# Attention of the second layer in a fused fp32 block: value product with split values stationary and two query blocks moving

## What is computed

```python
    def block(args):
        qn, qr = args
        s = (jnp.einsum('bqhd,bkhd->bhqk', qn, k_nope)
             + jnp.einsum('bqhd,bkd->bhqk', qr, k_rope)).astype(jnp.float32) * scale
        p = jax.nn.softmax(s, axis=-1).astype(v.dtype)
        return jnp.einsum('bhqk,bkhd->bqhd', p, v)
    ...
    y = o * jax.nn.silu(gate)
    return y @ w_out
```

## Time and profile before

| What | us |
|---|---|
| median of 3 runs (4584.55 to 4600.62) | 4598.31 |
| the profiled execution, its own time | 4581.67 |
| its span, first to last instruction | 4579.9 |
| PE busy (95% of the span) | 4337.8 |
| DVE busy | 1856.7 |
| ACT busy | 1277.5 |
| POOL busy | 1281.5 |
| the loop over blocks of the stage, from the first score matmul to the end of the last scores' issue (1191.1 to 1783.3) | 592.2 |
| from there to the first matmul of the output projection (1803.9) | 20.6 |

### The profile page before, as it was taken

How to read it: one execution, slowest core, us unless ns; L and a number is a source line. 1 busy time by engine, 2 the same in 40 slices (tenths; PEclk the granted TensorE clock), 3 DMA queues, 4 the chain that set the end, 5 groups by cost and what they waited for, 6 DMA issues and landing times.

```text
span 4579.9 us, 51693 instructions
## 1 busy us (share of the span) xinstructions
PE 4337.8 (95%) x20631; PEld 3531.6 (77%) x20631; DVE 1856.7 (41%) x3427; ACT 1277.5 (28%) x2692; POOL 1281.5 (28%) x1225
## 2 busy tenths in 40 slices
PE   8999999798999999899888999999999888999998
PEld 4969788477899998787556888887786566888887
DVE  2020210455355554612754343334514734333434
ACT  1120211213344443312543322112313533312222
POOL 1403120145100000632123444334332042433431
PEclk9959689699999999999988999999998998999999
DMA  5101012422100000310013111112210022111112
GB/s 184 54 23 42 23 37 70 145 96 69 41 7 8 8 8 28 104 48 23 1 44 102 46 56 47 47 46 70 97 43 13 1 67 98 48 47 44 56 49 97
DMA packets 224513, 244.67 MB, mean 53 GB/s; under 512 B 43848, under 2 KB 165208, under 8 KB 224272
## 3 DMA queue, kind: packets, MB, share of 16 engines
q1 hardware_dynamic: 190432, 162.78, 12.0%
q10 hardware_dynamic: 33840, 78.58, 4.9%
HBM read 209.10 MB, written 30.07 MB: 52 GB/s over the span
## 4 chain that ended last, share of the span: by engine, by line
PE 84%; DVE 9%; ACT 3%; issue 1%; DMA 1%; POOL 1%; SPq 0%; ACTq 0%; DVEq 0%; POOLq 0%
PE ps L127 79%; PE ps L130 5%; DVE tlo L139 1%; DVE cst_sm L150 1%; DVE tfi L147 1%; ACT m_junk L133 0%; POOL mix_z L139 0%; DVE m_hb L147 0%; ACT f_ta L133 0%; DVE m_z L147 0%; ACT thi L133 0%; DVE gt_yr L139 0%; DVE m_z L139 0%; DVE c_rn L139 0%; DVE tfl L147 0%
## 5 line engine op out<-in xcount | busy, mean ns | idle before, releaser
L136 POOL CAST whi<-wst 128x512 fp32r<-128x512 f32 (+3 forms) x562 | 389.9, 694 | 2767.0 <-DMA wst<-in_a_w_in 561.2
L139 POOL TENSOR_TENSOR wlo<-wst,whi 128x512 fp32r<-128x512 f32 (+3 forms) x562 | 733.7, 1306 | 45.0
L127 PE MATMUL ps<-thi,whi 128*128 128x512 f32 x1760 | 692.2, 393 | 14.0 <-ACT m_z L133 5.6
L127 PE MATMUL ps<-tlo,whi 128*128 128x512 f32 x1760 | 690.5, 392 | 0.0
L127 PE MATMUL ps<-thi,wlo 128*128 128x512 f32 x1760 | 689.8, 392 | 0.0
L127 PE MATMUL ps<-whi,thi 128*128 128x512 f32 (+3 forms) x1752 | 670.1, 382 | 3.5 <-DVE mix_z L139 2.6
L127 PE MATMUL ps<-wlo,thi 128*128 128x512 f32 (+3 forms) x1752 | 665.3, 380 | 0.0
L127 PE MATMUL ps<-whi,tlo 128*128 128x512 f32 (+3 forms) x1752 | 664.9, 379 | 0.0
L147 DVE SCALAR_TENSOR_TENSOR f_ta<-f_ua,tfi,f_ta 128x1024 f32<-128x1024 f32 x88 | 120.6, 1371 | 736.7 <-ACT f_ta L133 735.1
L127 PEld LDWEIGHTS ps<-whi,thi 128*128 128x128 f32 x1752 | 370.5, 211 | 50.7 <-DVE mix_z L139 3.0
L127 PEld LDWEIGHTS ps<-whi,tlo 128*128 128x128 f32 x1752 | 370.1, 211 | 47.3
(11 more groups left out here) (266 smaller groups left out, 6145.0 us busy)
## 6 DMA issues: line engine op xcount, KB each, us to landing
wst<-in_w_up SPq DMA_DIRECT2D x704, 64.0 KB, 2.0
wst<-in_ada_w SPq DMA_DIRECT2D x96, 256.0 KB, 3.6
wst<-in_w_down SPq DMA_DIRECT2D x88, 256.0 KB, 2.6
wst<-in_a_w_in SPq DMA_DIRECT2D x96, 192.0 KB, 2.4
wst<-in_w_in SPq DMA_DIRECT2D x64, 256.0 KB, 2.7
wst<-in_w_out SPq DMA_DIRECT2D x32, 256.0 KB, 4.6
m_xr<-scr_x ACTq DMA_DIRECT2D x16, 512.0 KB, 3.6
scr_x<-m_z ACTq DMA_DIRECT2D x16, 512.0 KB, 2.7
```

Source lines behind the costliest of these rows:

```text
L127: return self.none if self.e is None else self.e.matmul(*a, **k)
L136: return self.none if self.e is None else self.e.tensor_copy(*a)
L139: return self.none if self.e is None else self.e.tensor_tensor(*a)
```

## The change

- **Value product.** The values are stationary: for each 128 keys a 128x128 square with the 64 columns of the high part beside the 64 of the low part (`bv`). The transposed weights of two blocks, a pair, are moving, 256 columns wide, once their high part (`pth`) and once their low part (`ptl`): 16 matmuls of 128x256 in fp32r for a pair. The result is transposed, values by queries; rows 0 to 63 come from the high values, 64 to 127 from the low.
- **Evacuation of a turn.** ACT copies both halves (the high parts), and DVE subtracts for both halves (the low parts). Before, each engine copied one half.
- **Order.** The value product of a pair is issued in even iterations, behind that iteration's scores. A turn of an even block stands behind the value product, a turn of an odd block at the head of the next, odd iteration, in front of the scores.
- **Gate.** POOL multiplies the gate by the reciprocal of the sum (one 128x64 TENSOR_SCALAR a block). PE transposes two gate squares a pair into the bank of the output. ACT copies 64 rows of the bank (one half of the output, and the gate) to `ot`, DVE adds the other half, POOL multiplies by the gate into `tfl`. The output is then already transposed, so the 64 squares at the end go; 16 copies by ACT and 16 subtractions by DVE of 128x512 split it, and `pe_out` waits for the k-th of them at its k-th step.
- **Smaller.** The scale moves into the query table, so TENSOR_SCALAR goes and the maximum is written negated. The low part of a query piece is made by POOL and the queries have one buffer `qs` in place of two. Value pieces stand two iterations later and are split in two copies and two subtractions each. The waits for the gate's DMAs move from the start of ACT's and DVE's programs to the first low part of a turn. POOL splits 11 of the 16 weight tiles of the output projection within the loop.

```diff
-    c["k_qtab"] = tab
+    c["k_qtab"] = tab * f(96.0 ** -0.5)
...
+        self.bv = [[x[:, 4 * hf:4 * hf + 4, :] for hf in range(2)] for x in v] + [[four(self.thi[:, 7, half(hf)]) for hf in range(2)]]
+
+        self.pth = [four(self.thi[:, 8, :]), self.place("ml5_p0", [128, 4, 256], F32R, mod)[:]]
...
-                self.split(q, ("wo", st, h, k))
+                if st != "b" or 8 * h + k > 10:
+                    self.split(q, ("wo", st, h, k))
...
     def pool_heads(self, q):
-        for h in range(16):
+        S = self.S
+        for h in range(2):
             self.split(q, ("head", h))
+        for piece in self.first_pieces():
+            self.pool_piece_lo(q, *piece)
+        for i in range(128 + 7):
+            if i and self.piece_at(i - 1):
+                self.pool_piece_lo(q, *self.piece_at(i - 1))
+            if i % 8 == 0 and i < 112:
+                self.split(q, ("head", i // 8 + 2))
+            if i % 8 == 4 and 40 <= i < 128:
+                n = i // 8 - 5
+                self.split(q, ("wo", "b", n // 8, n % 8))
+            if i >= 5 and i % 2 == 1 and i < 133:
+                p = (i - 5) // 2
+                y, o, r = self.head_out(p)
+                q.wait_ge(*self.B.done(("bo", p)))
+                q.wait_ge(*S.last("b_gate"))
+                q.wait_ge(*S.last("w_lo"))
+                q.wait_ge(*S.last("lo_p"))
+                q.tensor_tensor(y, o[:, 0:256], o[:, 256:512], ALU.mult).then_inc(*S.up("b_y", p))
+                q.wait_ge(*S.at("b_y", p))
+            if 1 <= i < 129:
+                u = i - 1
+                h, j = u // 8, u % 8
+                g = self.tfl[:, h // 2 + 1, j * 128 + 64 - h % 2 * 64:j * 128 + 128 - h % 2 * 64]
+                q.wait_ge(*S.at("b_rec", u))
+                if h == 0:
+                    q.wait_ge(*S.at(f"ld_g{j}"))
+                q.tensor_scalar(g, g, self.bstat(u, 2), None, ALU.mult).then_inc(*S.up("b_gate", u))
...
     def pieces(self, h):
-        return [("q", 0), ("k", 0), ("q", 1), ("k", 1)] + ([("v", 0), ("v", 1)] if h % 2 == 0 else [])
+        return [("q", 0), ("k", 0), ("q", 1), ("k", 1)] + ([None, None, ("v", 0), ("v", 1)] if h % 2 == 0 else [])
...
+            for n in range(2):
+                if h + n >= 3:
+                    q.wait_ge(*S.at("pv", ("b", 4 * (h + n - 3) + 3)))
+                ins = q.activation(self.bv[(h + n) % 3][hf][:, :, 0:64], p.rearrange("p (a b) -> p a b", a=4)[:, :, 64 * n:64 * n + 64],
+                                   ACT.Copy)
+            ins.then_inc(*S.up("hi", key))
...
+            if (h, hf) != (0, 0):
+                q.wait_ge(*S.at("hi", ("piece", h if hf else h - 1, what, 1 - hf)))
+                q.wait_ge(*S.at("lo_p", ("hq", h if hf else h - 1, 1 - hf)))
+            q.tensor_tensor(self.qs[:], p, self.msh[:, r], ALU.mult).then_inc(*B.free(key, "evac_v"))
...
+        else:
+            q.wait_ge(*S.at("hi", key))
+            for n in range(2):
+                v = self.bv[(h + n) % 3][hf]
+                ins = q.tensor_tensor(v[:, :, 64:128], p.rearrange("p (a b) -> p a b", a=4)[:, :, 64 * n:64 * n + 64],
+                                      v[:, :, 0:64].bitcast(F32), ALU.subtract)
+            ins.then_inc(*B.free(key, "evac_v"))
...
+    def pool_piece_lo(self, q, h, what, hf):
...
-        q.tensor_tensor(self.ql[x][:, r], self.qs[hf][:], self.qh[x][:, r].bitcast(F32), ALU.subtract).then_inc(
-            *self.S.up("lo", ("hq", h, hf)))
+        q.tensor_tensor(self.ql[x][:, r], self.qs[:], self.qh[x][:, r].bitcast(F32), ALU.subtract).then_inc(
+            *self.S.up("lo_p", ("hq", h, hf)))
...
+        for i in range(128 + 4):
+            if i % 2 == 1 and i >= 3:
+                self.pe_head_turn(q, i - 2)
...
-            if 2 <= i < 130:
-                for n in range(2):
-                    self.pe_turn(q, ("bt", i - 2, n), [self.bp[(i - 2) % 3][:, blk(4 * n + k)] for k in range(4)], "t2",
-                                 [S.at("exp", ("b", i - 2))])
-            if i < 120 and i % 8 < len(self.pieces(i // 8 + 1)):
-                self.pe_piece(q, i // 8 + 1, *self.pieces(i // 8 + 1)[i % 8])
-            if 3 <= i < 131:
-                u = i - 3
-                h = u // 8
-                key = ("bo", u)
+            if i == 2:
+                self.pe_head_turn(q, 0)
+            if i >= 4 and i % 2 == 0:
+                p = (i - 4) // 2
+                h, n = p // 4, p % 4
+                key = ("bo", p)
                 b = B.take(key, "o2")
                 for event in B.freed(key):
                     q.wait_ge(*event)
-                v = self.bv[h // 2 % 2]
-                for k in range(8):
-                    q.wait_ge(*B.done(("bt", u, k // 4)))
-                    q.wait_ge(*B.done(("piece", h // 2 * 2, "v", k // 4)))
-                    ins = q.matmul(ps[:, b, 0:64], self.bpt[u % 2][:, blk(k)], v[:, k, h % 2 * 64:h % 2 * 64 + 64],
-                                   start=(k == 0), stop=(k == 7))
-                ins.then_inc(*S.up("pv", ("b", u)))
-        for j in range(8):
+                q.wait_ge(*S.at("b_gate", 2 * p + 1))
+                for k in range(2):
+                    q.transpose(ps[:, b, 256 + 128 * k:384 + 128 * k], self.tfl[:, h // 2 + 1, blk(2 * n + k)], self.ident[:])
+                for hf in range(2):
+                    q.wait_ge(*B.done(("bt", 2 * p + 1, hf)))
+                    q.wait_ge(*B.done(("piece", h // 2 * 2, "v", hf)))
+                    for k in range(4):
+                        v = self.bv[h % 3][hf][:, k, :]
+                        q.matmul(ps[:, b, 0:256], v, self.pth[hf][:, k, :], start=(hf == 0 and k == 0), stop=False)
+                        ins = q.matmul(ps[:, b, 0:256], v, self.ptl[hf][:, k, :], start=False, stop=(hf == 1 and k == 3))
+                ins.then_inc(*S.up("pv", ("b", p)))
+                self.pe_head_turn(q, i - 2)
+            if self.piece_at(i):
+                self.pe_piece(q, *self.piece_at(i))
+
+    def pe_head_turn(self, q, u):
+        if u < 128:
             for n in range(2):
-                y = self.tfi if n else self.tfl
-                self.pe_turn(q, ("T", "by", j, n), [y[:, k, blk(j)] for k in range(4)], "tr4",
-                             [B.done(("bo", 120 + j))])
+                self.pe_turn(q, ("bt", u, n), [self.bp[u % 3][:, blk(4 * n + k)] for k in range(4)], "t2",
+                             [self.S.at("exp", ("b", u))])
...
-                q.wait_ge(*S.at("turned", ("bt", u, 0)))
                 if u >= 2:
-                    q.wait_ge(*S.at("pv", ("b", u - 2)))
-                q.activation(self.bpt[u % 2][:, 0:512], ps[:, B.of(("bt", u, 0)), :], ACT.Copy).then_inc(
-                    *B.free(("bt", u, 0), "evac_a"))
-            if i < 120 and i % 8 < len(self.pieces(i // 8 + 1)):
-                self.act_piece(q, i // 8 + 1, *self.pieces(i // 8 + 1)[i % 8])
-        for j in range(8):
-            for n in range(2):
-                self.act_hi(q, ("T", "by", j, n), 4 * n, 4, j, [S.at("turned", ("T", "by", j, 1))])
+                    q.wait_ge(*S.at("pv", ("b", u // 2 - 1)))
+                for n in range(2):
+                    key = ("bt", u, n)
+                    q.wait_ge(*S.at("turned", key))
+                    q.activation(self.pth[n][:, :, u % 2 * 128:u % 2 * 128 + 128],
+                                 ps[:, B.of(key), :].rearrange("p (a b) -> p a b", a=4), ACT.Copy).then_inc(*S.up("hi", key))
+            if i >= 4 and i % 2 == 0:
+                p = (i - 4) // 2
+                r, o = 64 * (1 - p // 4 % 2), self.head_out(p)[1]
+                q.wait_ge(*S.at("pv", ("b", p)))
+                if p >= 2:
+                    q.wait_ge(*S.at("b_y", p - 2))
+                q.activation(o, ps[r:r + 64, B.of(("bo", p)), :], ACT.Copy).then_inc(*S.up("b_half", p))
+            if self.piece_at(i):
+                self.act_piece(q, *self.piece_at(i))
+        for kt, hf in self.Y_ORDER:
+            q.wait_ge(*S.at("b_y", 4 * (2 * kt + 1) + 2 * hf + 1))
+            q.wait_ge(*S.at("qk", ("b", 127)) if kt < 4 else S.at("turned", ("bt", 127, 1)) if kt < 7 else S.at("pv", ("b", 59)))
+            q.activation(self.thi[:, kt, half(hf)], self.tfl[:, kt, half(hf)], ACT.Copy).then_inc(*S.up("hi", ("by", kt, hf)))
...
-                q.tensor_reduce(self.bstat(i, 0), ps[:, b:b + 2, :].rearrange("p a b -> p (a b)"), AXX, ALU.max).then_inc(
-                    *S.up("v_seq"))
-                q.wait_ge(*S.last("v_seq"))
-                q.tensor_scalar(self.bstat(i, 1), self.bstat(i, 0), -scale, None, ALU.mult).then_inc(*S.up("b_max", i))
+                q.tensor_reduce(self.bstat(i, 0), ps[:, b:b + 2, :].rearrange("p a b -> p (a b)"), AXX, ALU.max,
+                                negate=True).then_inc(*S.up("b_max", i))
+            if 1 <= i < 129:
+                u = i - 1
+                q.wait_ge(*S.at("exp", ("b", u)))
```

(70 more changed lines are left out.)

85 lines of the change are left out of this document (43 added, 42 removed).

## The result

The changed kernel takes 4707.3 us (median of 4 runs, 4696.38 to 4719.52) against 4599.47 (4584.55 to 4602.83). The ratio is 1.0242, 95% interval 1.0203 to 1.0280: slower. The profiled execution took 4698.93 us by its own time, its span is 4697.1, and the mean granted clock over it is 0.93.

The account below looks back on a forecast made before the run. PE bounded the old loop; the change would replace that with a chain through ACT and DVE. Loop +104.7, start −3.0, end −6.7, clock +12 make +107 us: 4581.67 becomes 4689, with 16.6 for the median 4705; range 4660 to 4775.

Parts of the forecast that it names:

- The walk: One loop pair without pieces, followed link by link over PE, ACT and DVE: 10.63 us instead of 8.10.
- PE's work: PE's own work in a loop pair: 6.82 us in place of 8.10, with 128x256 matmuls 0.12 apart.
- Pieces: Pieces within the loop: 0.60 us more for each of 30 key pieces, 0.7 for each of 7 value pieces.
- Start: Start of the stage: waits for the gate's DMA move behind two blocks, −3.0 us.
- Clock: PE's idle waits in the loop let the clock fall to 1.2 GHz 7 times, +12 us.
- End: From the last odd scores to the output projection: 13.9 us, before 20.6, so −6.7.
- The sum: Loop, start, end and clock together: 104.7 − 3.0 − 6.7 + 12 = +107 us.
- about a third: Sign in the changed kernel's profile: share of the loop's chain of waits that ACT and DVE should hold between them.
- Most pairs with a fall: Rival, chance 0.13: the clock falls in most loop pairs, priced at 80 us instead of 12, about 4773.
- PE as the bound: Rival, chance 0.06: ACT's copies come before the exp in time, both PE waits close, −92 us, so 4506.
- one wait absent: Rival, chance 0.05: one of PE's two waits in a pair is missing, a pair takes 9.07 us, 4607.
- slower links: Rival, chance 0.06: links slower than their rows through POOL or semaphores, half a microsecond a pair, +32 us, 4737.

Follow-up runs that it names:

- e10: Changed kernel with DVE taking the maximum of each odd block twice, output unchanged; 4822.5 us, one run.
- e1: Changed kernel with ACT's copies and DVE's low parts of the previous turn ahead of the odd block's exp and maximum; 4625.2 us, ratio to before 1.0071.
- e11: Changed kernel with ACT copying each output twice and POOL taking each product with the gate twice; 4702.9 us, ratio to before 1.0238.
- e9: Changed kernel reordered: copies first, a block's scores between any two turns, key and query pieces moved on PE, ACT and DVE; 4524.6 us, ratio to before 0.9844.
- e7: Changed kernel with only DVE's part of a key piece put behind the next maximum; 4685.7 us, ratio to before 1.0193.
- e8: Changed kernel with ACT's and DVE's waits for the gate's DMAs back at the start of the stage; 4711.9 us, one run.
- e3: Changed kernel with the two gate transposes ahead of each value product issued five times over; 4690.8 us, ratio to before 1.0214.
- e6: e1 with DVE's part of a key piece put behind the next maximum; 4565.4 us, ratio to before 0.9927.
- e4: Changed kernel with four repeated 128x512 score matmuls ahead of the gate transposes before each value product; 4699.0 us, ratio to before 1.0224.

## Why the prediction was right, step by step

- **The walk.** Predicted and measured, from the moment when the odd scores are out (1487.12): maximum 0.20 and 0.24, exp 1.46 and 1.50, copies 2.57 and 2.60, value product 3.93 and 3.97, next maximum 4.39 and 4.43, even turn 5.85 and 5.99, odd turn 8.12 and 8.15, PE's first wait 2.24 and 2.16. The pair takes 10.63 and 10.59. Rows of the kernel before, put end to end, gave each of these to 0.14 us or better. e10 shows that the maximum is a link, e1 that the order makes it one, e11 that the output is none.
- **PE's work.** 128x256 matmuls start 0.12 apart, and the shortest pairs of e9 take 7.02 us for 6.82.
- **Pieces.** 0.60 a key piece: 11.2 a pair for 10.6, and e7's 18. An odd value piece's pair and the key pair behind it (no fall in either) take 11.87 + 10.65 = 22.52, so 1.34 over two plain pairs, for 0.7 + 0.6. POOL and query pieces cost nothing in the loop, as said.
- **Start.** −3.4 for −3.0, and e8 gives 3.3.
- **Clock.** 11 falls for 7, at 1.2 to 1.5 us for 1.7: some 15 for 12. That they would be few was a reading of the earlier trace rows near its lower end, and the number was a choice, not worked out. The links without them come to about 692, for 696.9.
- **End: mis-sized.** −4.4 for −6.7. The value product starts 3.9 behind the last scores, as forecast. But PE has then waited 3.55 us, and the value product runs at 1.2 GHz (granted clock 0.50 from 1903.1 to 1906.3):
```profile
1903.11 0.58 PE L127 MATMUL ps<-thi,ml_v 128*128 128x256 f32 x1 [3.55 <-DVE ml_p L139]
...
1910.68 0.39 PE L127 MATMUL ps<-thi,ml_v 128*128 128x256 f32 x1 [0.60 <-DVE ml_p L139]
...
1914.09 0.72 POOL L139 TENSOR_TENSOR tfl<-ml_o 64x256 f32<-64x256 f32 x1 [3.67 <-DVE ml_o L139]
1914.17 1.19 DVE L139 TENSOR_TENSOR tlo<-tfl,thi 128x512 fp32r<-128x512 f32 x1 [0.23 <-ACT thi L133]
...
1915.41 0.50 PE L127 MATMUL ps<-whi,thi 128*128 128x512 f32 x1 [2.56 <-DVE tlo L139]
```
  This value product takes 3.42 us instead of 1.92, and the last one begins 11.5 us behind the last scores instead of 9.85. The step had priced the clock for the loop and none for the end. Another 0.7 lies between it and the projection (4.73 for 4.05). Of this, 0.5 is DVE's first low part, for which PE waits: it lasts 1.19, and those behind it 0.68. It runs beside POOL's last product. In all 12 kernels with this end it lasts 1.19, and in e11, where a second product of POOL follows, the second low part is long too (1.22). The prediction's chain had counted on the 0.68 of the rows and on no POOL beside it.
- **The sum.** 107.2 us measured in the stage for +107. That it fits so closely is partly luck: loop −1.7, end +2.3, start −0.4. So is the 4707.3 for 4705: the profiled executions lie 117.3 apart, 10 more than the sum of 107, and the changed kernel's median lies 8.4 above its profiled execution, where the forecast took 16.6.
- **A marker that was wrong.** ACT and DVE were to hold "about a third" of the chain in the loop. They hold 59%. My own walk says so too: 3.93 us up to the value product and 2.3 up to the odd turn are 6.2 of 10.63. The figure was not worked out, and whoever had judged by it would have called a right theory wrong.
- **The rivals.** Most pairs with a fall (0.13): 11 of 63. By the rule in the Trainium skill, "TensorE: Matmul & The Clock Gate", section "PE-mode transpose", that transposes do not count as busy in the same way, this one would have been the likelier; here the traces disagree. With 8 more transposes in each wait before the value product (e3) none of the 10 falls behind it is left, and the loop of e9, where turns and gate transposes take about 2 of each 7 us, runs at 1.00. What transposes do with no matmuls near them, no run here shows. PE as the bound (0.06), one wait absent (0.05) and slower links (0.06) did not come. The first of these has its condition right: it asked for copies ahead of the exp, and e1 and e6 show that this is what decides between slower and faster. That the change allowed such an order was outside the forecast.

## What to carry to other kernels

Making the bound engine's work cheaper is worth nothing until the chain that hands it its operands is shorter too. Walk one period of the loop with every engine's instructions in their program order, put the durations end to end, and see which engine waits: with rows of the old kernel this gave the new period to 0.04 us. If a link stands behind an instruction that itself waits for something later (here a copy behind an exp, and a maximum behind a piece's low part), change the order before giving up the change: here reordering the same instructions turned 2.4% slower into 1.6% faster.

## What was not expected of the hardware

The clock did not fall at the same idle time each round. PE waits 2.16 us before the value product in 26 pairs of one and the same pattern, and 10 of these waits are followed by 3.4 us at 1.2 GHz. Nor do the traces give an idle time that is safe. The loop of e6, where PE waits at most 1.7 us, had no fall. But e3, e4, e8 and e11 have 2, 3, 1 and 1 falls behind waits of about 1.72 ahead of a turn, and each of these loops has 15 such waits. With waits of 1.9 to 3.3 before each value product (e10) there were 52 falls in 63 pairs. A stretch at low clock costs less than its length suggests: 3.4 us at half speed cost 1.0 to 1.5, as part of it lies in the next wait.

A subtraction on DVE took longer beside an instruction of POOL only where both its operands lay in SBUF. At the end of the stage, where it reads `tfl` and `thi`, it took 1.19 us, and 1.22 for the second one in e11, instead of 0.68. In the loop 35 subtractions that read a bank (`ml_p<-ps`) run beside POOL in the same way, and none takes more than 0.69. Why this is so was not tested.
